# Turned head outputs of the attention in the bank of the head products

## The reference

```
s = jnp.einsum('bhiqd,bhikd->bhiqk', qb, k) * (HEAD_DIM ** -0.5)
p = jax.nn.softmax(s, axis=-1)
p_diff = p[:, :, 0] - lam * p[:, :, 1]
o = jnp.einsum('bhqk,bhkd->bhqd', p_diff, v)
o = rmsnorm(o, g_subln) * (1.0 - lam_init)
```

## Time and profile before

| what | value |
|---|---|
| median of 3 runs | 2696.61 us (2695.8 to 2697.26) |
| profiled execution, its own time | 2699.22 us |
| its span, first to last instruction | 2697.4 us |
| busy: PE, PEld, DVE, ACT, POOL | 96%, 88%, 77%, 38%, 6% of the span |
| mean granted clock of TensorE | 0.987 |
| attention of layer 0, first scores to output projection | 789.89 to 897.85 us |
| attention of layer 1, the same | 2191.43 to 2273.02 us |

### The profile page before, as it was taken

The page is one execution under the profiler, slowest core; times in us unless marked ns, Lnnn a source line. Parts: engine busy times, 40 slices in busy tenths (PEclk is TensorE's granted clock), DMA queues, the critical chain, the costliest instruction groups (busy, mean ns, idle before and its releaser), DMA issues. The chain is left out here.

```text
span 2697.4 us, 42701 instructions
## 1 busy us (share of the span) xinstructions
PE 2587.2 (96%) x15352; PEld 2375.4 (88%) x15352; DVE 2079.5 (77%) x3420; ACT 1020.3 (38%) x1873; POOL 167.6 (6%) x316
## 2 busy tenths in 40 slices
PE   6999999999997999999999999999999987999998
PEld 4899999988955789999999799999997955889997
DVE  5698888888937478888888887777768856688886
ACT  4333432333147333332332434323324155344443
POOL 2000000020003210000000200000001013100001
PEclk7999999999999999999999999999999999999999
DMA  8134333332211112333334133333322211223331
GB/s 304 40 125 130 117 93 115 119 98 63 89 39 48 32 55 89 123 94 113 124 97 133 55 102 117 94 125 108 114 67 89 76 47 32 76 82 110 104 109 53
DMA packets 193241, 256.33 MB, mean 95 GB/s; under 512 B 7262, under 2 KB 130764, under 8 KB 193100
## 3 DMA queue, kind: packets, MB, share of 16 engines
q1 hardware_dynamic: 193100, 254.43, 29.5%
HBM read 252.31 MB, written 2.10 MB: 94 GB/s over the span
## 5 line engine op out<-in xcount | busy, mean ns | idle before, releaser
L1132 PE MATMUL ps<-h_hi,w_hi 128*128 128x384 f32 (+2 forms) x2368 | 792.3, 335 | 21.9 <-DVE h_lo L2150 19.4
L1134 PE MATMUL ps<-h_hi,w_lo 128*128 128x384 f32 (+2 forms) x2368 | 786.8, 332 | 0.0
L1133 PE MATMUL ps<-h_lo,w_hi 128*128 128x384 f32 (+2 forms) x2256 | 750.3, 333 | 0.0
L1132 PEld LDWEIGHTS ps<-h_hi,w_hi 128*128 128x128 f32 x2368 | 450.4, 190 | 54.1 <-issue 21.8
L1134 PEld LDWEIGHTS ps<-h_hi,w_lo 128*128 128x128 f32 x2368 | 450.4, 190 | 20.8
L1133 PEld LDWEIGHTS ps<-h_lo,w_hi 128*128 128x128 f32 x2256 | 429.0, 190 | 19.6 <-issue 1.0
L1663 ACT ACTIVATE w_hi<-raw 128x512 fp32r<-128x512 f32 x464 | 279.8, 626 | 419.1 <-PE ps L1134 325.8
L2282 DVE TENSOR_TENSOR w_lo<-raw,w_hi 128x512 fp32r<-128x512 f32 x464 | 307.3, 684 | 14.7 <-ACT w_hi L1663 14.7
L1132 PE MATMUL ps<-t_hi_all,w_hi 128*128 128x384 f32 x864 | 292.0, 338 | 0.0
L1134 PE MATMUL ps<-t_hi_all,w_lo 128*128 128x384 f32 x864 | 292.0, 338 | 0.0
L1133 PE MATMUL ps<-t_lo_all,w_hi 128*128 128x384 f32 x864 | 291.9, 338 | 0.0
(11 more groups left out here) (257 smaller groups left out, 4039.5 us busy)
## 6 DMA issues: line engine op xcount, KB each, us to landing
side_raw<-in_w_ada SPq DMA_DIRECT2D x240, 256.0 KB, 2.7
raw<-in_w_ffn_gate SPq DMA_DIRECT2D x44, 1024.0 KB, 5.4
raw<-in_w_ffn_up SPq DMA_DIRECT2D x44, 1024.0 KB, 5.4
raw<-in_w_ffn_down SPq DMA_DIRECT2D x44, 1024.0 KB, 5.0
raw<-in_w_in SPq DMA_DIRECT2D x14, 1024.0 KB, 5.3
ada_buf<-in_w_ada SPq DMA_DIRECT2D x12, 1024.0 KB, 12.7
raw<-in_w_out SPq DMA_DIRECT2D x8, 1024.0 KB, 5.1
raw<-in_w_in SPq DMA_DIRECT2D x8, 512.0 KB, 6.7
```

The costliest lines, as they stand in the source:

```text
L1132: mm(out, wh, xh, start=start, stop=False, skip_group_check=reopened)
L1133: mm(out, wh, xl, start=False, stop=False, skip_group_check=reopened)
L1134: return mm(out, wl, xh, start=False, stop=stop, skip_group_check=reopened)
```

## The change

The turned head outputs of the steps are booked in bank 7 in place of bank 6. The late ones stay as they are.

```diff
         for i in attention_steps(l):
             if 0 <= i - OT_LAG < len(u):
-                self.slot(("OT", l, i - OT_LAG), 6)
+                self.slot(("OT", l, i - OT_LAG), 7)
             if i < len(u):
```

## The result

The change is slower: 2717.08 us (median of 4 runs, 2713.15 to 2719.78) against 2696.94 us (median of 4); the ratio is 1.0066 with a 95% interval of 1.0055 to 1.0078. That is 20 us where 9.4 were forecast, and 3 us above the top of the range. The profiled execution took 2718.72 us with a span of 2716.9 us, 19.5 more than the span before.

The account below looks back on a forecast made before the run. A ring of waits, with no engine full, was taken to bound the steps; +7.0 us in layer 0 and +2.4 in layer 1 made +9.4 on the 2696.61 median: 2706.0 us, range 2700.5 to 2714.0.

Parts of the forecast that it names:

- OT waits for the copy of O; ring of 5.37 us: Latent steps behind latent ones: turned head output waits for VectorE's copy of unit i-4's head product; 5.37 us for 4.55.
- Context steps gain: Steps with context-unit scores: 3.41 us behind a latent unit, where one took 4.32, and 3.34 behind a context unit.
- Steps with splits: Steps with weight splits on VectorE or ScalarE: 5.81, 6.01, 5.86 us in layer 1; 6.35, 5.14 in layer 0.
- 0.26 from OT to S: On TensorE, scores start 0.26 us behind the turned head output, counted as part of each latent step's 5.37 us.
- The tails: Steps after the last scores, up to the output projection: 9.74 us in layer 0, 13.48 in layer 1.
- Four more of these: +5.4: Four more score products at TensorE's lower clock, 1.34 us each: +5.4 us, 2711.4 us in all, chance 0.20.
- the ring's general gap of 1.4 us: TensorE idle 1.4 us per latent step, from the second transposes' end near 3.7 to the turned head output at 5.11.
- The first rival: TensorE's clock falls oftener because of idle gaps; four more slow score products, +5.4 us, 2711.4 us, chance 0.20.
- the six slow scores: Six score products at half clock, 8.0 us on top of the forecast, setting the range's top of 2714.0 us.
- The shorter ring: Scores start with the turned head output, not 0.26 behind; latent steps 5.11 us, total 2700.8 us, chance 0.13.
- the faster case: Copy of O done before the second transposes end, near 3.7 us into the step; no new wait, 2688.0 us, chance 0.04.

Follow-up runs that it names:

- the wait alone: Kernel before (bank 6) with one wait added: each turned head output also waits for VectorE's copy of the head product of unit i-4; 2715.72 us, ratio 1.0061.
- The filled runs: The change with TensorE work repeated in layer 0, same values: from step 9 on, 2714.39 us; only in latent steps from step 12 on, 2711.13 us.
- The reordered versions: The change with VectorE's copy of O ahead of the combination: always, 2696.23 us; latent steps only, 2696.89; also layer 0's tail in bank 6, 2692.73.

## Why the prediction was right in kind and wrong in size

- *OT waits for the copy of O; ring of 5.37 us.* Right to 0.01: 5.37 to 5.40 in every latent step behind a latent one, of the profiles with this ring, that met neither a split nor the lower clock. VectorE's idle time ahead of the maxima, some 1.5 us in the prediction, is there in two parts: 0.82 us ahead of a_lo and only 0.75 for the scores. The run with the wait alone shows that the wait is the loss.
- *Context steps gain.* Right: 3.41 forecast, 3.41 and 3.40 measured in steps 10 and 22, behind latent units, and 3.50 for 3.34 behind a context unit. Step 16 took 4.28, see below.
- *Steps with splits.* Right within 0.3: layer 1's steps 9, 11 and 12 took 5.82, 5.85 and 5.82 (5.81, 6.01, 5.86); layer 0's steps 11 and 12 took 6.62 and 5.28 (6.35, 5.14).
- *0.26 from OT to S.* The row held: 2265.36 and 2265.61. The step from OT to S is 0.25 or 0.26 all along layer 1's ring in this profile.
- *The tails, a mis-sized term.* 9.74 forecast for layer 0, 11.36 measured, and 13.48 for 14.18 in layer 1. I priced a_lo at 1.12 us behind OT from a place where ScalarE was free. Behind the last scores it is not:

```profile
902.00 0.33 PE L1390 MATMUL ps<-ident,onorm 128*128 128x128 f32 x1
...
902.37 0.47 ACT L2008 ACTIVATE e<-ps,nb 128x256 f32<-128x256 f32 x1
...
902.82 0.37 ACT L2024 ACTIVATE h_hi<-ps,gsub 128x128 fp32r<-128x128 f32 x1
...
903.72 1.58 PE L1584 MATMUL ps<-vN,pT 128*128 128x128 f32 x12 [0.75 <-DVE a_lo L2780]
```

  ScalarE still makes an exponential, and the head product starts 1.72 us behind OT. Each later one of layer 0, and each in layer 1's tail, starts 1.26 or 1.27 behind it, since it follows a_lo's start by 0.49 us where the transposes of the earlier trace rows followed by 0.41, and h_hi starts 0.05 later behind OT too. Another tenth of a microsecond goes between such a product and the next OT. The tails are 2.3 us longer than summed; 0.4 of it is the clock, which was 0.61 in the last 2.1 us of layer 0's, and 1.9 is this term.
- *The clock, the step that failed.* "Four more of these: +5.4" with a chance of 0.20, and the forecast itself had no term for it. In the profile steps 14, 15, 16 and 21 of layer 0 cost 1.53 + 1.39 + 0.87 + 1.38 = 5.2 us more than the sum gave (step 16 itself ran at full clock, with its head product late behind the slow step 15), steps 13 and 20 another 0.3 at their ends, the tail the 0.4 above, and the projection behind the stretch 2.4, which I had not priced at all: 8.3 us in this profile. The filled runs show that TensorE's idle time is what brings the slow scores in these steps: the same ring with more work under it ran at 0.98 in place of 0.86, and the kernel took about 5 us less by the medians, with intervals that touch. I had used the ring's general gap of 1.4 us and said only that it is "more" behind context units. There it is 2.74, and it could have been added up: a head product of 0.61 in place of 1.50 and no second half of transposes. The first rival, not the forecast, is what happened; the six slow scores that make the range's top of 2714.0 left out what else runs at the lower clock. The sizes then add up: 9.4 forecast, 1.9 of the tails, 0.6 of steps 11, 12 and 17, and 8.3 of the clock are 20.2 us, my estimate from this one profile; its span is 19.5 us longer, and the medians differ by 20.1. In two other profiles with bank 7 in layer 0 its stretch was 3.5 and 4.2 us shorter, so how near this comes is in part chance.
- *The other rivals.* The shorter ring and the faster case both fell: with the change OT never started before the copy's end. Weight loads do run ahead of their products, by 0.11 us for the head product (2267.38 for 2267.49), but those of the scores start with them, at 2265.61, 0.25 behind OT. The prediction gives the shorter ring 2700.8 us, and 2700.5 as the end of the range. The point named for the faster case was an earlier copy. The reordered versions bring it, from 5.06 us into a latent step to 3.63 (848.39 to the copy's end at 852.02); OT still waits for it in layer 0's latent steps, and they do gain.

What the runs leave open is why the clock in layer 1's first nine steps is 1.00 in some profiles and 0.83 or 0.84 in others (36.7 and 41.2 us from first to tenth scores, with the same work), and why it differs at the program's end. Both widen the spread of all versions.

## What to carry to other kernels

Before a product is moved to another bank, write down who empties that bank and how late in its own queue: an engine that waits, ahead of its next work, for the far end of another engine's queue can turn two overlapping engines into one serial ring, whose length is the sum along it (5.38 us here for 4.55). Then add up TensorE's idle time in the emptiest step, not the mean one, and give the clock a term in the forecast where that gap grows. If the bank is wanted all the same, move the emptying forward in the other engine's queue (3.94 us here), and keep the old bank where nothing gains by the new one, as in the tail. Whether it pays to leave the emptying where it was in steps where its input comes late was tried and not resolved.

## What the runs showed of the hardware

Four profiles have this ring with nothing filled in (the change twice, bank 7 in layer 0 alone, the wait alone). In each, TensorE idles 2.74 or 2.75 us before OT of steps 14 and 20 in layer 0. In seven of these eight places the scores right behind it ran wholly or partly at the lower clock (2.32 to 2.93 us for 1.56; the granted clock was 0.50 over a product of 2.93 us and 0.64 over the one of 2.32); in the eighth the next step's did. With matmuls repeated in the gap, 1.63 us of it were left and all four such scores took 1.56. In layer 1's ring steps, from step 10 on with gaps of 1.15 to 1.42 us and full head products, the scores took 1.56 us in every profile; in its tail the clock fell in three of the six profiles with this ring there (head products of 2.32, 2.35 and 2.47 us).

The length of a gap alone does not settle it. In step 11 of layer 0 the head product ran at the lower clock, granted 0.50, behind 1.89 us of idle time with the change (2.90 us for 1.50), and behind 1.94 before (2.58). Step 9's scores did so in the kernel before behind 0.72 us (2.90), and with the change behind 1.23 in one profile (2.85) and not in another (1.56). No run here gives a gap at which the clock falls. Nor do gaps in every step bring it by themselves: layer 1's ring steps from step 10 on idle as regularly as layer 0's, and the granted clock was 1.00 up to the tail in all six profiles.
